# Two of four weight-sum sets of the seven-product slabs made on GpSimd in place of VectorE

## The reference

```
h = rms(x, norm_g)
hq, hf, hi, hgate, dq, dk, dv, iq, ik, iw, dgate, nq, nck, ncv, nsk, nsv, nwk, nwv, ... = split(h @ w_in)
y_a = hgrn2(hq, hf, hi) * silu(hgate)                 # gated linear recurrence
y_b = dsa(rope(dq), rope(iq), iw, keys, index_rows)   # top-k chosen by an indexer
y_c = nsa(rope(nq), compressed, selected, window)     # three attention branches
y = x + sum(sigmoid(m) * (y_i @ w_branch_i)) @ w_out
```

## Time and profile before

| What | us |
|---|---|
| median of 3 runs | 931.21 |
| lowest and highest of them | 927.59, 931.62 |
| the profiled execution | 930.0 |
| its span in the profile | 928.3 |

### The profile page before, as it was taken

The page is one execution under the profiler, slowest core; times in us unless marked ns, Lnnn a source line. Parts: engine busy times, 40 slices in busy tenths (PEclk is TensorE's granted clock), DMA queues, the critical chain, the costliest instruction groups (busy, mean ns, idle before and its releaser), DMA issues.

```text
span 928.3 us, 17646 instructions
## 1 busy us (share of the span) xinstructions
PE 911.3 (98%) x6444; PEld 748.0 (81%) x6444; DVE 525.5 (57%) x1472; ACT 299.2 (32%) x643; POOL 129.7 (14%) x258
## 2 busy tenths in 40 slices
PE   9999999999999999999999999999999999999998
PEld 7998778877777787888899887778677867777887
DVE  4863678876744675034357455898675536731331
ACT  3136433246632113400120553422666321242000
POOL 0420000002033361000070000000200503600000
PEclk9999999999999999999999999999999999999999
DMA  7654456317199798344465445643343988963432
GB/s 280 238 177 148 163 231 249 115 58 273 46 324 384 279 385 297 108 149 163 136 202 183 148 139 198 249 182 128 121 173 125 377 308 314 380 221 131 136 136 93
DMA packets 56792, 189.02 MB, mean 204 GB/s; under 512 B 9218, under 2 KB 22914, under 8 KB 44418
## 3 DMA queue, kind: packets, MB, share of 16 engines
q1 hardware_dynamic: 43426, 138.56, 42.5%
q0 software_dynamic: 12992, 49.16, 14.2%
q10 hardware_dynamic: 288, 0.18, 0.1%
HBM read 177.47 MB, written 18.77 MB: 211 GB/s over the span
## 4 chain that ended last, share of the span: by engine, by line
PE 80%; DVE 7%; ACT 4%; DVEq 3%; DMA 2%; issue 2%; SPq 2%; ACTq 0%
PE ps L1100 16%; PE ps L901 15%; PE ps L1422 9%; PE ps L920 5%; PE ps L1316 5%; PE ps L1434 3%; PE ps L1428 3%; PE ps L913 3%; DMA slab<-in_weights_dram 2%; PE ps L1221 2%; PE ps L1396 2%; PE ps L1210 2%; DVE arena L2053 1%; PE ps L1295 1%; PE ps L1188 1%
## 5 line engine op out<-in xcount | busy, mean ns | idle before, releaser
L901 PE MATMUL ps<-hT,slab 128*128 128x264 f32 (+1 forms) x928 | 214.5, 388 | 0.0
L901 PEld LDWEIGHTS ps<-hT,slab 128*128 128x128 f32 (+1 forms) x928 | 174.0, 190 | 30.9 <-issue 1.1
L1100 PE MATMUL ps<-hT,slab 128*128 128x264 f32 x736 | 174.1, 393 | 1.4 <-DMA slab<-in_weights_dram 0.8
L1100 PEld LDWEIGHTS ps<-hT,slab 128*128 128x128 f32 x736 | 138.3, 192 | 31.6 <-DVEq L2207 3.2
L1446 ACT ACTIVATE arena<-ps 128x512 f32<-128x512 f32 (+20 forms) x142 | 65.8, 491 | 149.0 <-PE ps L1316 47.2
L1422 PE MATMUL ps<-Y,slab 128*128 128x264 f32 x384 | 85.8, 386 | 0.0
L1422 PEld LDWEIGHTS ps<-Y,slab 128*128 128x128 f32 x384 | 72.8, 190 | 12.3
L1316 PEld LDWEIGHTS ps<-arena,w 128*128 128x128 f32 x512 | 58.4, 192 | 10.0 <-issue 6.6
L1316 PE MATMUL ps<-arena,w 128*128 128x128 f32 x512 | 61.4, 278 | 0.0
L619 POOL DMA_DIRECT2D arena<-in_pages_kv_dram x64 | 33.3, 520 | 153.4 <-DVEq L2437 115.3
L628 POOL DMA_DIRECT2D arena<-in_pages_kv_dram x64 | 35.0, 547 | 99.1 <-PE ps L1316 27.0
(11 more groups left out here) (394 smaller groups left out, 1366.4 us busy)
## 6 DMA issues: line engine op xcount, KB each, us to landing
slab<-in_weights_dram SPq DMA_DIRECT2D x84, 1024.0 KB, 5.1
arena<-in_pages_kv_dram SPq DMA_DIRECT2D x64, 256.0 KB, 8.4
arena<-in_pages_kv_dram POOLq DMA_DIRECT2D x64, 256.0 KB, 6.9
arena<-in_pages_kv_dram POOLq DMA_DIRECT2D x64, 128.0 KB, 8.2
arena<-in_pages_kv_dram SPq DMA_DIRECT2D x64, 128.0 KB, 11.7
out_dram<-in_state_win_dram POOLq DMA_DIRECT2D x2, 4088.0 KB, 23.6
arena<-in_state_hgrn_dram SPq DMA_DIRECT2D x2, 2048.0 KB, 12.0
out_dram<-arena POOLq DMA_DIRECT2D x2, 2048.0 KB, 8.9
```

What stands on the lines that cost most here:

```text
L901: last = mm(ps[0:job[3], n % 2, 0:LT], v[:, k, job[2]:job[2] + job[3]], hT[:, k, :], start=(k == 0), stop=(k == KD - 1))
L1100: last = mm(ps[:, bank, 0:LT], v[:, k, (d % 2) * 128:(d % 2) * 128 + 128], hT[:, k, :], start=(k == 0), stop=(k == KD - 1))
```

## The change

The sums of slabs 2 and 3 (n3 and dq0) move from VectorE to GpSimd. There they stand behind the requests for the first pair's index rows and ahead of the requests for the other three pairs, in both layers. GpSimd waits for the slab and for "b 0" or "b 1", does the same four operations with the same three drains, and counts a semaphore of its own, `sv_g`, for which TensorE waits ahead of the product with s2. On VectorE `sums_of(i + 2)` falls away, and the wait inside it.

```diff
--- before.py
+++ after.py
@@ -510,7 +510,8 @@
         grp_v = Steps("grp_v", ["zr iq", "zr k", "zr dq", "zr nq"])
         N7 = range(len(SEVEN))
         sv_p = Steps("sv_p", [f"{b} {i}" for i in N7 for b in "abc"])
-        sv_v = Steps("sv_v", ["T", "S 0", "S 1"] + sum([[f"a {i}", f"b {i}", f"c {i}"] + [f"S {i + 2}"] * (i + 2 < len(SEVEN)) for i in N7], []))
+        sv_v = Steps("sv_v", ["T", "S 0", "S 1"] + sum([[f"a {i}", f"b {i}", f"c {i}"]  for i in N7], []))
+        sv_g = Steps("sv_g", [f"S {i}" for i in N7[2:]])
         rows_p = Steps("rows_p", ["rows"])
         rows_a = Steps("rows_a", ["rows"])
         pidx_p = Steps("pidx_p", ["iw"] + [f"dot {h}" for h in range(NH)])
@@ -783,6 +784,19 @@
                 l1 = bass.ds(l, 1)
                 pool.wait_ge(x_ready, l + 1)
                 load_index_keys(pool, l, 0, pages)
+                for i in N7[2:]:
+                    slot, _, dmas = SLOT_AT[SEVEN[i]]
+                    pool.wait_ge(slab_in[slot], (l * SLOT_DMAS[slot] + dmas) * 16)
+                    pool.wait_ge(sv_p.sem, sv_p(l, f"b {i - 2}"))
+                    a11, a12, a21, a22 = blocks_of(i)
+                    x = SS7[i % 2]
+                    nc.gpsimd.tensor_tensor(x[:, 0], a21, a22, ALU.add)
+                    pool.drain()
+                    nc.gpsimd.tensor_tensor(a21, a11, a21, ALU.subtract)
+                    nc.gpsimd.tensor_tensor(x[:, 1], x[:, 0], a11, ALU.subtract)
+                    pool.drain()
+                    nc.gpsimd.tensor_tensor(x[:, 2], a12, x[:, 1], ALU.subtract)
+                    pool.drain().then_inc(sv_g.sem, sv_g.mark(f"S {i}"))
                 load_index_keys(pool, l, 1, pages)
                 load_index_keys(pool, l, 2, pages)
                 load_index_keys(pool, l, 3, pages)
@@ -936,7 +950,10 @@
                         pe.wait_ge(sv_v.sem, sv_v(l, f"c {i - 2}"))
                     product(a[:, 0], a11, b11)
                     product(a[:, 1], a12, b21)
-                    pe.wait_ge(sv_v.sem, sv_v(l, f"S {i}"))
+                    if i < 2:
+                        pe.wait_ge(sv_v.sem, sv_v(l, f"S {i}"))
+                    else:
+                        pe.wait_ge(sv_g.sem, sv_g(l, f"S {i}"))
                     product(a[:, 2], s2, TS7[:, 1]).then_inc(sv_p.sem, sv_p.mark(f"a {i}"))
                     product(b[:, 0], s1, TS7[:, 0])
                     product(b[:, 1], a21, TS7[:, 2])
@@ -1859,8 +1876,6 @@
 
                     slot, _, dmas = SLOT_AT[SEVEN[i]]
                     ve.wait_ge(slab_in[slot], (l * SLOT_DMAS[slot] + dmas) * 16)
-                    if i >= 2:
-                        ve.wait_ge(sv_p.sem, sv_p(l, f"b {i - 2}"))
                     a11, a12, a21, a22 = blocks_of(i)
                     x = SS7[i % 2]
                     TT(x[:, 0], a21, a22, ALU.add)
@@ -1916,8 +1931,6 @@
                         TT(zq, kept, turned, ALU.add).then_inc(grp_v.sem, grp_v.mark("zr iq"))
                     second_bank(i)
                     third_bank(i)
-                    if i + 2 < len(SEVEN):
-                        sums_of(i + 2)
 
                 for name in ("k", "dq", "nq"):
                     z, n, normed, cols = GROUPS[name]
```

## The result

The changed kernel takes 941.78 us (median of 4 runs, 940.85 to 944.18) against 930.87 for the kernel before on the same chip (median of 4): a ratio of 1.0118, 95% interval 1.0089 to 1.0147. The forecast was 931.9 with a range up to 937.0, so time and range were both wrong; the direction alone was right. The profiled execution has a span of 940.3 us, 12.0 above that of before.

The account below looks back on a forecast made before the run. The prediction took TensorE, busy 98% of the span, as the bound, with VectorE's sums hidden. One 1.9 us stall in layer 0, all else 0, on the profiled 930.0 us gave 931.9, range 928.5 to 937.0.

Parts of the forecast that it names:

- What bounds the kernel, and the worth of VectorE's relief: Seven-product slabs are unbroken TensorE work, 25.20 us per layer; taking two 2.96 us sets per layer off VectorE gains 0.
- The sums: Each 128x512 sum on GpSimd takes 1.17 us, the middle of 0.96 and 1.39; wider ends 0.69 and 1.86.
- When a set can start: In layer 0 GpSimd's eight first-pair requests, 0.59 us each from 35.47, decide: the first set starts at 40.19.
- The drains: Three GpSimd drains inside each set of sums cost 0.10 us each, so a set takes 5.0 us.
- Layer 1, "cost 0": In layer 1 the sums are ready at 497.7 and 503.5, before TensorE wants them at 501.13 and 507.43; cost 0.
- The stall's price: TensorE stands once, ahead of the third slab's third product in layer 0: 1.8 us, with the semaphore 1.9.
- Beside VectorE: GpSimd's first sums meet VectorE's two rotary steps in layer 0, costing 0.5 us; bounds 0 and 2.0.
- The rival of whole turns: GpSimd sums and VectorE rotary steps exclude each other for whole operations: 1.7 us rather than 0.5, total 933.1; chance 0.27.
- The queue behind GpSimd's waits: The other three pairs' 24 requests run later, to about 65 us in layer 0 and 517 in layer 1; cost 0.
- The range: From 928.5, no stall with a faster run, to 937.0, slow sums plus 0.8 us for run spread.
- slow sums: GpSimd sums take 1.86 us, a set 7.74; TensorE stalls in both layers, 6.2 us together, total 936.2; chance 0.14.

Follow-up runs that it names:

- the kernel that kept TensorE busy: The changed kernel with 16 unread matmuls per layer on TensorE ahead of its wait for the third slab's sums; 939.56 us, ratio 1.0081.
- the kernel with its own semaphore: The changed kernel with the three drains of each set replaced by waits on a semaphore that the sums raise; 933.44 us, ratio 1.0014.

## Why the prediction was wrong

- **What bounds the kernel, and the worth of VectorE's relief.** Right. With the sums on GpSimd and out of the way, the stretches are 25.20 us as before and the time is the same.
- **The sums.** Right within 8%: 1.26 us measured, 1.17 taken between 0.96 and 1.39.
- **When a set can start.** Right: GpSimd's own requests decide, eight in 4.68 us against 8 x 0.59 = 4.72. In this execution they began at 34.20 rather than 35.47, so the first sum began at 39.00 rather than 40.19.
- **The drains: the step that failed.** "The three drains inside a set: VectorE shows 0.08 us, the gap in GpSimd's request stream 0.39; I take 0.10 each." The second measured 0.14 (from the third sum's end at 45.84 to the fourth's start at 45.98), the third 0.24 with the next set's waits. The first cost 3.09 us in layer 0 and 6.78 in layer 1, outside both bounds. The step priced a drain without the requests ahead of it; the experiments show that the price comes from the requests since the last drain, 0.08 us each, and from the wait for a late landing. TensorE's waits became 4.01 and 3.55 us where 1.9 and none were forecast. The rows were there, 6.57 and 11.17 us on line 811: the bounds came from another engine's drain and from a gap, when the same instruction on the same engine stood in the trace.
- **Layer 1, "cost 0".** This fell with it, and layer 1 had the bigger hole since 81 requests stood behind its drain. Without the drains layer 1 has no wait, as the step said.
- **The stall's price.** The sum took TensorE's idle time as the whole loss and put the clock behind it at nothing, without a reason. The lowered clock added some 3 and 1.7 us (7.09 - 4.01 and 5.32 - 3.55 in the changed kernel's own trace, 2.81 and 1.65 by the kernel that kept TensorE busy). No rival had this.
- **Beside VectorE.** The rival of whole turns was the right mechanism, and the forecast's 0.5 us the wrong size: the first two sums took 0.80 and 0.65 us longer, 1.45 together, in the kernel with its own semaphore. That kernel measured 933.4 where the rival gave 933.1; but in its profiled execution the stretch of layer 0 is 4.2 us longer (58.19 - 28.79 against 25.20), 2.7 of it the wait and 1.5 the clock, so part of the agreement is luck. In the changed kernel itself the turn fell on VectorE (its rotary step took 1.82 us rather than 0.99), for which nothing waits. The Trainium skill, SBUF — State Buffer, section "Who interferes with whom", has this rule, and the trace agrees: 1.90 us for a step of 0.99 that came second.
- **The queue behind GpSimd's waits.** Right: the 24 requests ran from 53.53 us on in layer 0, and no wait for index rows appeared.
- **The range.** It was built from the price of a sum. Its upper case, slow sums, was the wrong mechanism, and its 936.2 was passed. That sum also leaves out, in layer 1, the 0.5 us for VectorE that it has in layer 0: with it the sets are ready at 500.4 and 508.2, and the total is 936.7.

## What to carry to other kernels

A drain on an engine that also issues DMA requests is not the drain of an engine that only computes: count the requests since its last one, and order arithmetic that someone waits for ahead of them or by a semaphore of its own. Look up a synchronising instruction by its own line in the trace, as timelines and busy times leave it out. And a stall of a few us on TensorE costs more than its length when the granted clock falls behind it.

## What the runs showed of the hardware that was not expected

- A GpSimd drain costs 0.08 us per earlier request when all have landed (32: 2.69 us, 105: 8.63, none: 0.03 to 0.05). Where the last landing came late, it ended some 0.04 us per request after that: 0.38 us with 8 requests in the changed kernel, 1.56 us with 37 on line 811 in layer 0 of the kernel before (landing at 217.33, end at 218.89). Why a landed request still costs time is not known from these runs.
- Four idle times of TensorE of 2.5 to 3.9 us in these stretches were each followed by a granted clock of 0.50 (means of 0.50 to 0.58 over the windows behind them), in three of them for about 3 us and in one for 6; with 16 matmuls in their place it stayed at 1.00.
- A GpSimd sum and a VectorE operation with two inputs in on-chip memory ran in turns, each for a whole instruction, in whichever order they came: VectorE's steps of 0.99 us took 1.82 and 1.90, GpSimd's sums of 1.26 us 2.06 and 1.91.
